# A hybrid attention and delta-rule encoder step on one Trainium2 core: the prologue's loads and products in another order, the samples' top-k rounds spread over the core, and delta values scaled before the convolution taps

## The reference, cut to what matters

```python
mod = jax.nn.silu(c) @ w_mod + b_mod                     # 9 x 1024: shift, scale, gate, three times
x = x + 0.5*gt1 * swiglu(modulate(rms_norm(x, norm_ffn1), sh1, sc1), gate, up, down)   # FFN1, 2816 features
x = x + gt2 * hybrid_mixer(modulate(rms_norm(x, norm_mix), sh2, sc2), ...)             # mixer
x = x + 0.5*gt3 * swiglu(modulate(rms_norm(x, norm_ffn2), sh3, sc3), gate, up, down)   # FFN2
y = rms_norm(x, norm_final)

# in the mixer, after one combined projection w_in:
_, idx = lax.top_k(score, n_top)          # 128 of up to 512 keys for a prompt row, 68 of 272 for a sample row
p = softmax(logits + bias over the chosen keys)          # sparse attention
qkv = silu(causal_conv(concat([gq, gk, gv]), conv_w))    # 4 taps
v = v * beta                                             # "delta values" of the gated delta rule
# chunks of 64: (I + m) is inverted, then states are carried from chunk to chunk
```

## Time and profile before

| | |
|---|---|
| median of 3 runs | 1536.74 us (1530.62 to 1539.36) |
| profiled execution, its own time | 1530.79 us |
| its span in the trace | 1529.0 us, so 1.8 us lie around it |
| TensorE busy | 94% of the span |
| VectorE, ScalarE, GpSimd busy | 58%, 38%, 26% |

### The profile page before, as it was taken

The page is one execution under the profiler, slowest core; times in us unless marked ns, Lnnn a source line. Parts: engine busy times, 40 slices in busy tenths (PEclk is TensorE's granted clock), DMA queues, the critical chain, the costliest instruction groups (busy, mean ns, idle before and its releaser), DMA issues. The chain is left out here.

```text
span 1529.0 us, 28532 instructions
## 1 busy us (share of the span) xinstructions
PE 1444.5 (94%) x11426; PEld 1347.8 (88%) x11430; DVE 885.2 (58%) x1637; ACT 573.9 (38%) x1130; POOL 394.7 (26%) x360
## 2 busy tenths in 40 slices
PE   6899999999999999998997889898999999999996
PEld 3799999999999889997895668698999999999995
DVE  2646664575467451675576666563557458754863
ACT  2632431332334253544324423532544124422443
POOL 1702422330231240531002030112622034302400
PEclk9899999999999999999998999999999999999998
DMA  9434444445453223222107020232113312331221
GB/s 344 131 109 146 135 155 132 138 159 159 125 165 100 70 58 89 79 69 56 42 1 153 10 88 17 70 105 83 56 42 97 97 56 84 97 97 49 84 77 69
DMA packets 211736, 148.76 MB, mean 97 GB/s; under 512 B 18075, under 2 KB 190396, under 8 KB 211608
## 3 DMA queue, kind: packets, MB, share of 16 engines
q1 hardware_dynamic: 206264, 129.15, 28.9%
q0 software_dynamic: 5344, 17.81, 3.7%
HBM read 139.99 MB, written 6.95 MB: 96 GB/s over the span
## 5 line engine op out<-in xcount | busy, mean ns | idle before, releaser
L1005 PE MATMUL pair<-b_hi,w_hi 128*128 128x320 f32 x720 | 224.3, 312 | 0.0
L1005 PE MATMUL pair<-b_hi,w_lo 128*128 128x320 f32 x720 | 222.5, 309 | 0.0
L1005 PE MATMUL pair<-b_lo,w_hi 128*128 128x320 f32 x720 | 222.4, 309 | 0.0
L1075 PE MATMUL pair<-act_hi,w_hi 128*128 128x320 f32 x704 | 161.8, 311 | 0.0
L1075 PE MATMUL pair<-act_hi,w_lo 128*128 128x320 f32 x704 | 160.5, 309 | 0.0
L1075 PE MATMUL pair<-act_lo,w_hi 128*128 128x320 f32 x704 | 160.3, 309 | 0.0
L471 DVE SCALAR_TENSOR_TENSOR x_t<-pair,gate,x_t 128x320 f32<-128x320 f32 (+1 forms) x128 | 56.0, 479 | 168.0 <-PE pair L1075 142.3
L1005 PEld LDWEIGHTS pair<-b_hi,w_hi 128*128 128x128 f32 x720 | 135.1, 188 | 14.3 <-DVE w_lo L594 8.4
L588 ACT ACTIVATE w_hi<-sums_a 128x512 fp32r<-128x512 f32 x72 | 45.1, 627 | 251.9 <-POOL sums_a L622 132.0
L890 DVE TENSOR_TENSOR uvw<-pair,uvw 128x320 f32<-128x320 f32 (+1 forms) x126 | 67.6, 537 | 123.0 <-PE pair L1005 122.6
L1005 PEld LDWEIGHTS pair<-b_lo,w_hi 128*128 128x128 f32 x720 | 135.2, 188 | 0.0
(11 more groups left out here) (424 smaller groups left out, 3124.4 us busy)
## 6 DMA issues: line engine op xcount, KB each, us to landing
w_mod_raw<-w_mod SPq DMA_DIRECT2D x28, 1024.0 KB, 5.8
w_raw<-ffn_w_gate SPq DMA_DIRECT2D x40, 512.0 KB, 4.0
raw_more<-ffn_w_up SPq DMA_DIRECT2D x40, 512.0 KB, 3.8
w_raw<-w_in SPq DMA_DIRECT2D x24, 512.0 KB, 3.7
w_raw<-ffn_w_down SPq DMA_DIRECT2D x16, 384.0 KB, 3.2
raw_more<-ffn_w_down SPq DMA_DIRECT2D x16, 384.0 KB, 3.1
w_mod_a<-w_mod POOLq DMA_DIRECT2D x4, 1024.0 KB, 10.9
w_mod_b<-w_mod POOLq DMA_DIRECT2D x4, 1024.0 KB, 24.2
```

The costliest lines, as they stand in the source:

```text
L1005: mm = pe.matmul(job_bank(j, BANK_OF[part]), w[:, at, kk], mv[:, kk, s], start=(kk == 0 and v == 0 and part in FIRST_OF_BANK), stop=(kk == ...
L1075: mm = pe.matmul(pair[part % 2][:, b, 0:HALF], w[:, slot, k], mv[:, k, b * HALF:(b + 1) * HALF], start=(k == 0 and v == 0), stop=(k == n - ...
```

## The change

Three edits, made together.

1. **Prologue.** All first transfers go through SyncE's queue, in the order x, rows, `w_mod` for two steps, the two weights of units 0 and 1, `w_mod` for the other two, the next two weights. The four steps take the tiles in the order of `FIRST_TILES`: first half of scale, first half of shift, second halves. `amp` is made in halves (`dve_first_amp`). x is turned before any product with `w_mod`. The modulated x is made tile by tile in plain order, 0 to 3 with the first half tables, 4 to 7 with the second. On TensorE, steps 2 and 3 stand between the first k steps of units 0 and 1, and unit 2 (which now lies in banks 2 and 3) has its first four k steps ahead of the second half of units 0 and 1, and its last four behind.
2. **Samples' rounds.** The scores of the samples go to the free tail of `v_f`, and the 8 rounds and the mask of job 3 move from ahead of the core into its levels: 2 rounds at level (0,0), 1 at each of (0,1) to (0,3), 2 ahead of (1,0), 1 in (1,0), the rest and the mask in (1,2). The loads of the bias rows and the first attention job wait for four masks instead of five.
3. **Delta values.** `place_v` stands ahead of the taps of its step, not behind its scores.

```diff
+FIRST_TILES = (KD, 0, KD + KD // 2, KD // 2)
...
+        def dve_first_amp(dve, half):
+
+            ms = slice(KD // 2 * half, KD // 2 * half + KD // 2)
+            dve.wait_ge(mod_placed, KD + KD * half)
+            dve.tensor_scalar(amp[:, 0, ms], mod[:, KD + ms.start:KD + ms.stop], 1.0, None, ALU.add).then_inc(tables_done, 1)
+            dve.wait_ge(tables_done, 2 * half + 1)
+            gain = cols_a[:, R_GAIN + ms.start:R_GAIN + ms.stop]
+            dve.tensor_tensor(amp[:, 0, ms], amp[:, 0, ms], gain.unsqueeze(2).broadcast_to([P, KD // 2, NC_ROWS]),
+                              ALU.mult).then_inc(tables_done, 1)
...
+            def act_first_modulate(act, row_out):
+                for half in range(2):
+                    act.wait_ge(tables_done, 2 * half + 2)
+                    for m in range(KH * half, KH * half + KH):
+                        act.wait_ge(t_done, m + 1)
+                        act.activation(b_rows(m, slice(0, SEQ)), b_rows(m, slice(0, SEQ)), ACT.Identity,
+                                       scale=amp[:, 0, m, 0:1], bias=mod[:, m, 0:1]).then_inc(hp_done, 1)
+                        act.wait_ge(hp_done, m + 1)
+                        act.wait_ge(hs_done, m + 1)
+                        for src, hi, _ in b_split(m):
+                            ins = act.activation(hi, src, ACT.Copy)
+                        ins.then_inc(h_hi_done, 1)
+                    if half == 0:
+                        row_out(3, 2)
+                        early_hi(act, 2)
+                        row_out(4, 3)
...
+            def dve_first_modulate(dve, place_tiles):
+                for m in range(KH):
+                    times(m)
+                early_lo(dve, 0)
+                place_tiles(1, FIRST_TILES[1])
+                dve_first_amp(dve, 0)
+                early_lo(dve, 1)
+                for m in range(KH):
+                    lo(m)
+                    times(KH + m)
+                    if m == 2:
+                        place_tiles(2, FIRST_TILES[2])
+                early_lo(dve, 2)
+                place_tiles(3, FIRST_TILES[3])
+                dve_first_amp(dve, 1)
+                for m in range(KH, KD):
+                    lo(m)
...
+                if first:
+                    first_rows, turn_step = first_steps
+                    both_units(0, 0)
+                    both_units(1, 1)
+                    first_rows(2)
+                    both_units(2, 2)
+                    turn_step(2)
+                    first_rows(3)
+                    both_units(3, 3)
+                    turn_step(3)
+                    whole_begun(2)
+                    for k in range(KH):
+                        whole_step(2, k, k)
+                    for k in range(KH, KD):
+                        both_units(k, k)
+                    mods_after(1)
+                    for k in range(KH, KD):
+                        whole_step(2, k, k)
+                    mods_after(2)
...
-            for n in range(FIRST_MODS // 2):
-                t, half = 4 * (n // 2), n % 2
-                pool.dma_start(first_part(n), w_mod[:, 4 * half:4 * half + 4, t * P:(t + 4) * P]).then_inc(first_in[n // 2], 16)
...
             act.activation(ss_tok[:, 1], ss_tok[:, 0], ACT.Sqrt, scale=1.0 / D, bias=EPS).then_inc(std_done, 2)
-            row_out(3, 2)
-            row_out(4, 3)
+            row_out(1, 0)
             for u in range(RAW):
                 ffn1.early_hi(act, u)
-            ffn1.act_modulate(act)
+            row_out(2, 1)
+            ffn1.act_modulate(act, row_out)
...
+                if 0 <= v - V["g", 10] < GH:
+                    place_v(v - V["g", 10], 0)
+                    place_v(v - V["g", 10], 1)
                 if kind == "g":
                     x = x_conv[:, i % 2]
...
-                if 0 <= v - V["g", 10] < GH:
-                    place_v(v - V["g", 10], 0)
-                    place_v(v - V["g", 10], 1)
-
-                if v >= SCORE_V + IDX_HEADS // PER_STEP and (any(left[0:3]) or any(left) and v >= SAMPLE_V + NB // 2):
+                if v >= SCORE_V + IDX_HEADS // PER_STEP and any(left[0:3]):
                     next_rounds(2 if v <= V["g", 11] else 1 if v <= V["aq", 1] else 6)
-            while any(left):
+            while any(left[0:3]):
                 next_rounds(4)
+            sample_scores()
...
                 level_masked(0, lv)
                 biased(j)
+                sample_rounds(1 if lv else 2)
                 matrices(lv + 1)
...
-            level(1, 0, lambda: w_out(0))
+            sample_rounds(2)
+            level(1, 0, both((sample_rounds, 1), (w_out, 0)))
             level(1, 1, None, place_own)
-            level(1, 2, lambda: new_v(0))
+            level(1, 2, both((sample_mask,), (new_v, 0)))
```

More of the change, by code:

```diff
@@ new lines, in pool_first_modulate, with rows @@
+            def pool_first_modulate(pool):
+                def rows(t, m):
+                    return t[:, m, 1:NC_ROWS].unsqueeze(2).broadcast_to([P, NB, TB])
+                for m in range(KD):
+                    if m % KH == 0:
+                        pool.wait_ge(tables_done, 2 * (m // KH) + 2)
+                    pool.wait_ge(t_done, m + 1)
+                    s = ts_[:, m % 2].rearrange("p (b t) -> p b t", b=NB)
+                    x = b_rows(m, slice(SEQ, TOK)).rearrange("p (b t) -> p b t", b=NB)
+                    if m >= 2:
+                        pool.wait_ge(hs_done, m - 1)
+                    pool.tensor_tensor(s, x, rows(amp[:, 0], m), ALU.mult).then_inc(hs_part, 1)
+                    pool.wait_ge(hs_part, m + 1)
+                    pool.tensor_tensor(x, s, rows(mod, m), ALU.add).then_inc(hs_done, 1)
+                token_sums(pool, [KH + kk + 1 for kk in range(KH)])
@@ L750, in pool_modulate_halves @@
                         pool.wait_ge(hs_done, g - 1)
-                    elif not first:
+                    else:
                         pool.wait_ge(x_done, X_OUT + KD)
@@ L788, in load_weights @@
                         loaded = 1
-                    if v == 2 and first:
+                    if v in (0, RAW) and first:
+                        first_mods(v)
+                        first_mods(v + 1)
+                    if v == RAW and first:
                         sp.wait_ge(turned, SUMS0)
@@ L869, in act_halves @@
                                 act.wait_ge(act_lo_done, KEPT0 + f - 1)
-                            act.activation(row(f % 2).rearrange("p (a b) -> p a b", a=2), pair[0][:, :, 0:HALF],
-                                           ACT.Silu).then_inc(silu_done, 2)
+                            if first and j == 2:
+                                for b in range(2):
+                                    act.activation(row(1)[:, b * HALF:(b + 1) * HALF], bank[2 + b][:, 0:HALF], ACT.Silu).then_inc(silu_done, 1)
+                            else:
+                                act.activation(row(f % 2).rearrange("p (a b) -> p a b", a=2), pair[0][:, :, 0:HALF],
+                                               ACT.Silu).then_inc(silu_done, 2)
                             act.wait_ge(silu_done, SILU0 + 2 * f + 2)
@@ L1033, in pe_halves, with whole_banks, whole_begun @@
-                whole_product((0, 1), M_ORDER, True)
+                def whole_banks(i):
+                    if first and i == 2:
+                        return [bank[2 + b][:, 0:HALF] for b in range(2)]
+                    return [pair[i % 2][:, b, 0:HALF] for b in range(2)]
+                def whole_begun(i):
+                    pe.wait_ge(lo_done, LO0 + end_of["unit", i, 0])
+                    if first and i == 2:
+                        pe.wait_ge(t_done, KD)
+                    else:
+                        pe.wait_ge(pair_free[i % 2], FREE0 + i // 2)
@@ new lines, in whole_step @@
+                def whole_step(i, k, n_):
+                    slot = half_slot(end_of["unit", i, 0] - 2) // 2
+                    for v, (w, lo_) in enumerate(((w_hi, 0), (w_hi, 1), (w_lo, 0))):
+                        bb = (bhi, blo)[lo_]
+                        for b, dst in enumerate(whole_banks(i)):
+                            if k < KH:
+                                mv = (b12h, b12l)[lo_][:, k] if b else bb[:, k, B11]
+                            else:
+                                mv = bb[:, k - KH, B22 if b else B21]
+                            mm = pe.matmul(dst, w[:, slot, k], mv, start=(n_ == 0 and v == 0), stop=(n_ == KD - 1 and v == 2))
+                    if n_ == KD - 1:
+                        mm.then_inc(unit_done, 2)
@@ L1835, in make_mask @@
             def make_mask(job):
[L1836 removed]
+                s = score_of(job)
                 at = MASK_AT[job + 1]
@@ L2868, in _, with first_mods @@
             sp.dma_start(const[:, 0:CONST_FIRST], a["const_table"][:, 0:CONST_FIRST]).then_inc(c_rows_in, 16)
+            def first_mods(s):
+                w_mod = a["w_mod"][0].rearrange("(k p) f -> p k f", p=P)
+                for half in range(2):
```

(5 more changed lines are left out.)

206 lines of the change are left out of this document (92 added, 114 removed).

## The result

| | before | changed |
|---|---|---|
| median | 1536.9 us (6 runs, 1530.62 to 1539.36) | 1518.2 us (6 runs, 1517.31 to 1524.13) |
| profiled execution, its own time | 1530.79 us | 1519.01 us |
| its span | 1529.0 us | 1517.2 us |

The ratio is 0.9895, 95% interval 0.9874 to 0.9917: 18.7 us less by medians (12.8 to 19.4 by the interval), and 1517 was forecast. Between the two profiled executions it is only 11.8 us, where the sum of the prediction was 18.9. So the sum has to be looked at term by term.

What follows compares the result with a forecast made beforehand. TensorE, busy 94% of the span, was taken as the bound, losing time in waits and at its low clock. Terms -6.8 - 6.5 - 5.6 = -18.9 gave 1511.9 profiled, 1517.8 median, stated as 1517; range 1507 to 1527.

Steps and rivals of the forecast that it cites:

- the sum of the prediction: Whole kernel: the three edits' terms, -6.8 - 6.5 - 5.6 = -18.9 us, take the profiled execution from 1530.8 to 1511.9.
- Edit 1, forecast -6.8: Prologue: FFN1 starts at 32.6 instead of 44.85, unit 2 ends at 64.0 instead of 70.8, if transfers never starve.
- the two `w_lo` splits partly fall earlier, and I take 3.3: Prologue: from half an `amp` at 29.3 to FFN1's first product takes 3.3 us, against 4.3 before from `amp`.
- 31.4 were summed: Prologue: TensorE's work from FFN1's first product at 32.6 to the end of unit 2, 31.4 us.
- The bound of -9.5: Prologue: edit 1's best case, -9.5 us, if the low clock at the start does not recur.
- Edit 3, forecast -5.6: Delta values: both `v_beta` waits go, 4.1 us, and the low clock behind the longer one, 1.6; bounds -5.8 and -1.4.
- Edit 2, forecast -6.5: Core: samples' rounds fit VectorE's idle stretches and the `inv` wait goes; -7.4 + 0.4 + 0.5 = -6.5 us.
- forecast -7.4: Core, level (0,0): `m_mat` of the second tile moves from 823.20 to 815.8, 7.4 us earlier.
- the bound of -1.7: Core: edit 2's poorest case, -1.7 us, if GpSimd's products stretch the first two rounds 2.7 times, 4.8 us longer.
- the 1.5 that the prediction allowed: Core: sign to check for edit 2, no more than 1.5 us added to the `logit` waits.
- From each place on TensorE is fed as before, so the gains carry to the end.: Whole kernel: claims all three terms, -18.9 us in sum, last to the end of the execution.
- TensorE's clock in the core: Core levels: rival that new waits of 2 to 3 us hold the clock at 1.2 GHz; +8 us, 1545; chance 0.04.

Runs made afterwards that it cites:

- g2: Changed kernel with second step's row copy ahead of weight splits, half the tables ahead of first `w_lo`, 36 idle transposes on TensorE: 1515.96 us, ratio 0.9883.
- h1: Changed kernel with g2's prologue, 62 idle transposes in six `logit` waits of the core, and more at both FFN-mixer hand-overs: 1506.08 us, ratio 0.9818.
- in the second: The changed kernel measured again, beside the kernel before on another chip: 1516.51 us against 1532.04, ratio 0.9887.
- filled kernel: Changed kernel with 62 unread transposes in six `logit` waits: 1511.43 us, ratio 0.9857; likewise without edit 2, with 50 more ahead of `inv`: 1517.55, ratio 0.9896.

## Why the prediction was right, and where it was not

The number, the range and the sign were right: 1517 against 1518.2. That it came this near is luck in part: two errors of 6 to 7 us cancel (last step below). The steps:

**Edit 1, forecast -6.8, measured -5.2 in the trace at unit 3, of which 4.2 reach the mixer, and -6.2 (5.1 to 9.2 by the interval) as a change by itself.** x in at 11.33 (forecast "10.7 to 11"), half amp written at 29.4 (29.3): the chain of transfers and hand-overs was right to half a us. The step that was mis-sized is "the two `w_lo` splits partly fall earlier, and I take 3.3": it took 4.2. GpSimd's first product with `amp` started at 29.53 beside the second `w_lo` and took 1.32 us, the later ones 0.40. From the first product to unit 3 it took 32.0 us where 31.4 were summed. The low clock at the start recurred, over the first 6.0 us of products. The bound of -9.5 "if the low clock at the start does not recur" was nearly reached: g2 and h1 kept the clock and came to 61.7 to 62.0, 8.9 to 9.2 earlier than before, but only with the two reorderings.

**Edit 3, forecast -5.6, measured -5.6 in the trace (the entry of the core moves by -9.8, the mixer's first product with `conv_rows`, 561.76 before and 557.58 now, by -4.2), -6.7 by itself.** Both waits are gone, a wait of 0.3 for `v_beta` is left at another product (713.85), and the clock is 1.00 from 700 to 750. Here every step held.

**Edit 2, forecast -6.5.** The wait for `inv` vanished, and the first level product came 7.0 us closer to the entry. `m_mat` of the second tile starts 11.6 us behind the entry instead of 19.2: -7.5 (forecast -7.4). The scans did not stretch (0.44 and 0.43), so the bound of -1.7 was empty. The row it was taken from was misread, too: when `inv` took its 1.14 us (817.26), GpSimd was issuing transfers and began its four products only at 818.03. A product of GpSimd (813.51 to 814.55) lay beside the first `m_mat`, which took 1.22 us at 813.61. The `logit` waits grew by 2.3 us, more than the 1.5 that the prediction allowed. With the clock kept the edit gives 6.0 to 6.8. What failed is a sentence that followed the sum: "From each place on TensorE is fed as before, so the gains carry to the end." It was fed as before, and still ran at half its clock for longer: 5.6 us went that way in the core. I had this mechanism as the rival "TensorE's clock in the core", with the same places (a wait of 2 to 3 us at level (0,0)), at 0.04 and only in the size that makes the kernel slower. It should have been a term of 2 to 6 us with a wide range.

**The last step, from the profile to the median.** I set the sum (1511.9) against the profiled execution and added the 6 us by which that lay under the median. The changed kernel's profiled execution lies at its median, 1519.01. That execution of before had 58 us at the low clock where the 34 executions on another chip have 71.5 on average; at 0.31 us each this is 4.2 of the 6 us. So the sum was 7.1 too low for the pair of profiles, the offset was not carried over, and the two errors cancel in the 1517. By medians the three edits gave 18.7 in the first comparison and 15.5 in the second, and the single edits 17.6: the forecast 18.9 was high by 0.2 to 3.4.

What stays open: why the stretch near 885 lasts 20 us in edits 1 and 3 together and 7 in the changed kernel, which has the same wait ahead of it. That long stretch is where those two edits lost most. The filled kernels show that the low clock in the core needs the idle stretches; they do not show why the same wait is followed by it in one execution and not in another, nor what sets its length, nor why it fell at the hand-overs of h1 behind 0.3 us of idle time.

## What to carry to other kernels

Cost a removed wait in TensorE's time at its full clock, and then look for the idle stretches that stay behind it: stretches of 1.6 to 3.2 us were followed by 3.4 to 20 us at 1.2 GHz here, though not each time, so it is a term of its own with a wide range. Where TensorE waits anyway, work that nobody reads can keep its clock (it gained 5 us here); it brings nothing where the next engine's tiles set the pace. Before setting a sum against a profile, compare its mean granted clock with that of the other executions.

## What the hardware did that I had not expected

- TensorE's low clock followed idle stretches as short as 1.6 us in the core, and 0.32 us between products of one column at a hand-over, and lasted 3.4 to 20 us. One us at it cost 0.31 us of span on average in the kernel before. The Trainium skill (TensorE: Matmul & The Clock Gate, Terms) puts the penalty at the throttled time times the share of the clock that is missing, here one half. It was nil for the 6.8 us filled at each hand-over, and 0.4 in the core (the filled kernel against the changed one: 8.1 us between traces for 20.4 us at the low clock; 5.1 by medians).
- A `TENSOR_TENSOR` of VectorE on two SBUF tiles took 2.05 us beside four products of GpSimd, not 0.42, and a `TENSOR_SCALAR` 1.29, not 0.49; in the other direction GpSimd's product took 1.32 instead of 0.40 beside `w_lo`. `MAX8` and `MATCH_REPLACE8` did not change.
